# Joining the high and low part of a product's moving operand in one 512-column matmul, for three of seven products

## The reference

```python
xn = rms_norm(h, norm1_w[l])
proj = xn @ w_in[l] + b_in[l]
...
merged = jax.nn.sigmoid(gate_a) * (ya @ w_branch_a[l]) + jax.nn.sigmoid(gate_b) * (yb @ w_branch_b[l])
h = h + merged @ w_out[l]
xn2 = rms_norm(h, norm2_w[l])
h = h + (jax.nn.silu(xn2 @ w_ffn_gate[l]) * (xn2 @ w_ffn_up[l])) @ w_ffn_down[l]
```

## Time and profile before

| | |
|---|---|
| median of three runs | 816.99 us |
| profiled execution, span from first to last instruction | 815.2 us |
| TensorE busy | 808.4 us (99%), 5504 matmul records |
| VectorE busy | 539.7 us (66%), 561 instructions |
| ScalarE busy | 440.4 us (54%), 501 instructions |
| GpSimd busy | 414.0 us (51%), 146 instructions |
| granted TensorE clock | 0.999 |

### The profile page before, as it was taken

One profiled execution on the slowest core, in us unless ns is written; L12 is line 12 of the kernel. 1 busy time (PEld: TensorE's weight loads), 2 busy tenths in 40 slices (PEclk: granted clock), 3 DMA queues, 4 the chain that ended last, 5 costly groups with the idle time before them and its releaser, 6 DMA issues.

```text
span 815.2 us, 13365 instructions
## 1 busy us (share of the span) xinstructions
PE 808.4 (99%) x5504; PEld 750.1 (92%) x5504; DVE 539.7 (66%) x561; ACT 440.4 (54%) x501; POOL 414.0 (51%) x146
## 2 busy tenths in 40 slices
PE   9999999999999999999999999999999999999997
PEld 7888888888888899999998899999999999999985
DVE  5377377374674867888873278766667777677736
ACT  5523446665665645866542584454444446665624
POOL 4445424424224543477954543544444445978880
PEclk9999999999999999999999999999999999999999
DMA  7973523121123253322234203423234445535022
GB/s 294 265 263 115 164 95 104 52 104 57 52 98 115 95 204 105 104 104 105 103 130 185 104 1 107 152 106 109 106 111 159 159 152 186 178 125 212 1 78 104
DMA packets 27565, 103.11 MB, mean 126 GB/s; under 512 B 2816, under 2 KB 4224, under 8 KB 23552
## 3 DMA queue, kind: packets, MB, share of 16 engines
q1 hardware_dynamic: 22288, 87.07, 29.8%
q10 hardware_dynamic: 5232, 15.40, 5.9%
HBM read 94.08 MB, written 8.39 MB: 126 GB/s over the span
## 4 chain that ended last, share of the span: by engine, by line
PE 99%; DMA 0%; ACT 0%; issue 0%; SPq 0%; DVE 0%; ACTq 0%
PE acc L2109 14%; PE acc L2112 14%; PE acc L2111 14%; PE acc L1894 7%; PE acc L1896 6%; PE acc L1895 6%; PE acc L1913 6%; PE acc L1912 6%; PE acc L1911 6%; PE acc L2308 3%; PE acc L2307 3%; PE acc L2305 3%; PE acc L1940 3%; PE acc L2023 1%; PE acc L2062 1%; PE acc L2067 1%
## 5 line engine op out<-in xcount | busy, mean ns | idle before, releaser
L465 POOL TENSOR_TENSOR w_lo<-raw,w_hi 128x2048 fp32r<-128x2048 f32 x26 | 123.1, 4733 | 163.1 <-ACT w_hi L660 163.1
L486 POOL TENSOR_TENSOR A_lo<-wp,A_hi 128x1024 fp32r<-128x1024 f32 x51 | 126.1, 2472 | 145.6 <-ACT A_hi L833 137.3
L848 ACT ACTIVATE S_hi<-acc 128x1024 fp32r<-128x1024 f32 x68 | 68.1, 1024 | 89.5 <-PE acc L2112 56.3
L2112 PE MATMUL acc<-xt_hi,A_lo 128*128 128x256 f32 x408 | 115.5, 283 | 0.0
L2111 PE MATMUL acc<-xt_lo,A_hi 128*128 128x256 f32 x408 | 115.5, 283 | 0.0
L2109 PE MATMUL acc<-xt_hi,A_hi 128*128 128x256 f32 x408 | 115.5, 283 | 0.0
L1444 DVE TENSOR_TENSOR S_lo<-acc,S_hi 128x1024 fp32r<-128x1024 f32 x68 | 81.8, 1220 | 18.6 <-ACT S_hi L848 18.6
L1894 PE MATMUL acc<-xt_hi,w_hi 128*128 128x512 f32 (+1 forms) x240 | 92.5, 385 | 0.0
L1896 PE MATMUL acc<-xt_hi,w_lo 128*128 128x512 f32 (+1 forms) x240 | 91.7, 382 | 0.0
L1895 PE MATMUL acc<-xt_lo,w_hi 128*128 128x512 f32 (+1 forms) x240 | 91.7, 382 | 0.0
L660 ACT ACTIVATE w_hi<-raw 128x2048 fp32r<-128x2048 f32 x26 | 49.5, 1909 | 64.1 <-PE acc L1913 43.3
(11 more groups left out here) (323 smaller groups left out, 2337.6 us busy)
## 6 DMA issues: line engine op xcount, KB each, us to landing
wp<-wstream SPq DMA_DIRECT2D x34, 1024.0 KB, 6.9
raw<-wstream SPq DMA_DIRECT2D x26, 1024.0 KB, 4.8
wd<-wstream SPq DMA_DIRECT2D x16, 512.0 KB, 6.3
down_sums<-act_sum ACTq DMA_DIRECT2D x8, 512.0 KB, 3.6
sum_raw<-down_sums SPq DMA_DIRECT2D x8, 512.0 KB, 3.3
xn_in<-x ACTq DMA_DIRECT2D x4, 512.0 KB, 8.2
turned_sums<-tx ACTq DMA_DIRECT2D x4, 512.0 KB, 3.8
raw_out<-wstream SPq DMA_DIRECT2D x2, 1024.0 KB, 5.8
```

Source lines behind the costliest of these rows:

```text
L465: pool.tensor_tensor(w_lo[s][:, :], raw[s][:, :], w_hi[s][:, :], ALU.subtract).then_inc(lo_ready, 1)
L486: pool.tensor_tensor(low_of(name, rows), weights_of(name, c, rows), high_of(name, rows), ALU.subtract).then_inc(plain_low, 1)
L848: a.activation(high_of(name, rows), src, ACT.Copy).then_inc(op_high, 1)
L2112: mm = pe.matmul(dst, wl[:, g, k, :], x[0][:, k, :], start=False, stop=(k == 3), skip_group_check=True)
```

## The change

For the products S2, S3 and A22 of every pair but pair 8 (the first of the feed-forward), the two matmuls that have the same weights, high x high and high x low, become one matmul of 512 moving columns: the high part's 256 columns and the low part's 256 columns. To allow that, high and low parts are now two halves of one tensor. The result fills a whole bank for each of the two column groups: high sums in the first 256 columns, low sums in the last 256. The third matmul still has 256 columns and adds to the first half. S2 goes to banks 6 and 7 (where the weight difference stood before), S3 and A22 to banks 1 and 2, S1 and S4 to bank 3.

```diff
+            def wide_product(name, x, banks, start):
+
+                wh, wl = op_hi[name], op_lo[name]
+                for g in range(2):
+                    both = halves_of(bank[banks[g]])
+                    for k in range(4):
+                        pe.matmul(both, wh[:, g, k, :], x[:, :, k, :], start=(start and k == 0), stop=False,
+                                  skip_group_check=True)
+                        mm = pe.matmul(both[:, 0, :], wl[:, g, k, :], x[:, 0, k, :], start=False, stop=(k == 3),
+                                       skip_group_check=True)
+                mm.then_inc(product_done, 1)
...
-                product("S1", mt1, 2, True)
-
-                pe.wait_ge(s_low, 4 * p + ((2 if p == 1 else 3) - 4))
+                product("S1", mt1, 3, True)
+
+                pe.wait_ge(s_low, 4 * p - 1)
...
-                product("S2", mt2, 1, True)
+                wide_product("S2", mt2, (6, 7), True)
...
-                product("S3", mt3, 3, True)
+                wide_product("S3", mt3, (1, 2), True)
...
-                product("A22", t4, 3, False)
+                wide_product("A22", t4, (1, 2), False)
...
-                product("S4", x22, 2, False)
+                product("S4", x22, 3, False)
```

In the down pairs the weights are the moving operand, and `wide_down_product` does the same with them. The joins of these three products become two additions, the second of which waits for the first:

```diff
+            def join_wide(dst, banks, other, joins):
+
+                v.tensor_tensor(dst, low_sums(banks), other, ALU.add).then_inc(part_joined, 1)
+                v.wait_ge(part_joined, joins)
+                return v.tensor_tensor(dst, high_sums(banks), dst, ALU.add)
...
-                v.tensor_tensor(mu2[:, :], bank[1][:, :], mp1[:, :], ALU.add).then_inc(joined, 1)
+                join_wide(halves_of(mu2), SECOND_SUM, halves_of(mp1), JOINS * p + (1 - JOINS)).then_inc(joined, 1)
...
-                v.tensor_tensor(u3[:, :], bank[3][:, :], mu2[:, :], ALU.add).then_inc(joined, 1)
+                join_wide(halves_of(u3), LAST_ROW, halves_of(mu2), JOINS * p + (2 - JOINS)).then_inc(joined, 1)
...
-                merge_quarter(2, 3, mu2).then_inc(joined, 1)
+                join_wide(mcq[:, 2, :, :], LAST_ROW, halves_of(mu2), JOINS * p).then_inc(joined, 1)
```

ScalarE's copy of A21 for the next pair waits for U2's join, since it writes the banks that S2 now stands in, and the output block and the first down block wait also for c21:

```diff
+                if u2 is not None:
+                    a.wait_ge(joined, u2)
                 a.activation(row_diff if rows else diff, weights_of("A21", c, rows), ACT.Copy).then_inc(a21_copied, 1)
...
                         pe.wait_ge(taken, 2 * MERGE_PAIRS)
+                        pe.wait_ge(joined, 5 * MERGE_PAIRS - 1)
```

More of the change, by code:

```diff
@@ L97 @@
 FIRST_SUMS = 6
+JOINS = 3
 WARM_UP = 10
@@ L130, in build @@
         mt_raw = [sb(f"mt_raw{n}", 84 + 8 * n, [P, 4, HT]) for n in range(3)]
-        mt_hi = [sb(f"mt_hi{n}", 80 + 8 * n, [P, 4, HT], F32R) for n in range(3)]
-        mt_lo = [sb(f"mt_lo{n}", 84 + 8 * n, [P, 4, HT], F32R) for n in range(3)]
+        mt = [sb(f"mt{n}", 80 + 8 * n, [P, 2, 4, HT], F32R) for n in range(3)]
+        mt_hi, mt_lo = ([t[:, part, :, :] for t in mt] for part in range(2))
         mt4 = sb("mt4", 104, [P, 4, HT])
@@ L181, in build @@
         wd = [sb(f"wd{c}", 16 * c, [P, KD, HALF]) for c in range(2)]
-        row_hi = {n: sb(f"{n}_row_hi", kb, [P, 4, HT], F32R) for n, kb in SLOT.items()}
-        row_lo = {n: sb(f"{n}_row_lo", kb + 4, [P, 4, HT], F32R) for n, kb in SLOT.items()}
+        row = {n: sb(f"{n}_row", kb, [P, 2, 4, HT], F32R) for n, kb in SLOT.items()}
+        row_hi, row_lo = ({n: t[:, part, :, :] for n, t in row.items()} for part in range(2))
         def high_of(name, rows):
@@ L1078, in pair @@
                 a.wait_ge(s_low, at(p, 4, 1 - 4))
-                a21_copy(1 - c, nn, rows)
+                a21_copy(1 - c, nn, rows, None if first else at(p, 5, 1 - 5))
                 a11_high(1 - c, nn, rows)
@@ L2270, in pair @@
                     pe.wait_ge(sil_ready, 2)
-                product("S2", t2, 1, True)
+                if first:
+                    product("S2", t2, 1, True)
+                else:
+                    wide_product("S2", t2, (6, 7), True)
                 pe.wait_ge(s_low, p * 4 + (3 - 4))
@@ L2276, in pair @@
                     pe.wait_ge(act_ready, 2)
-                product("S3", t3, 3, True)
+                if first:
+                    product("S3", t3, 2, True)
+                else:
+                    wide_product("S3", t3, (1, 2), True)
                 pe.wait_ge(plain_low, p * 3 - 1)
@@ L2286, in pair @@
                     pe.wait_ge(t_low, N_LOW + 4)
-                product("A22", t4, 3, False)
+                if first:
+                    product("A22", t4, 2, False)
+                else:
+                    wide_product("A22", t4, (1, 2), False)
                 pe.wait_ge(s_low, p * 4)
                 pe.wait_ge(joined, p * 5 + (3 - 5))
-                product("S4", x22, 2, False)
+                product("S4", x22, 3, False)
             pair(MERGE_PAIRS + 1, True)
@@ L2304, in down_product, with wide_down_product @@
                     for k in range(4):
-                        pe.matmul(dst, x[0][:, k, ts], wh[:, k, :], start=(start and t == 0 and k == 0), stop=False,
+                        pe.matmul(dst, x[:, 0, k, ts], wh[:, k, :], start=(start and t == 0 and k == 0), stop=False,
                                   skip_group_check=True)
-                        pe.matmul(dst, x[0][:, k, ts], wl[:, k, :], start=False, stop=False, skip_group_check=True)
-                        mm = pe.matmul(dst, x[1][:, k, ts], wh[:, k, :], start=False, stop=(k == 3),
+                        pe.matmul(dst, x[:, 0, k, ts], wl[:, k, :], start=False, stop=False, skip_group_check=True)
+                        mm = pe.matmul(dst, x[:, 1, k, ts], wh[:, k, :], start=False, stop=(k == 3),
+                                       skip_group_check=True)
+                mm.then_inc(product_done, 1)
+            def wide_down_product(name, x, banks, start):
+                for t in range(2):
+                    both = halves_of(bank[banks[t]])
+                    ts = slice(t * P, (t + 1) * P)
+                    for k in range(4):
+                        pe.matmul(both, x[:, 0, k, ts], row[name][:, :, k, :], start=(start and k == 0), stop=False,
+                                  skip_group_check=True)
+                        mm = pe.matmul(both[:, 0, :], x[:, 1, k, ts], row_hi[name][:, k, :], start=False, stop=(k == 3),
                                        skip_group_check=True)
```

96 lines of the change are left out of this document (56 added, 40 removed).

## The result

The changed kernel took 827.6 us (median of 4 runs, 826.46 to 830.36) against 816.93 us for the kernel before on the same chip (816.86 to 817.32). The ratio is 1.013, with a 95% interval of 1.0115 to 1.0145: 10.7 us slower, where 6.4 us were worked out and 823.0 was forecast. The direction was right. The time lies 0.1 us outside the range given, and 4.6 us above the forecast.

The account below looks back on a forecast made before the run. TensorE was taken to bound the kernel, with 99% of the chain of waits. 816.99 us plus 12.8 of stalls less 6.4 saved gave 823.4, rounded down to 823.0; range 817.5 to 827.5.

Parts of the forecast that it names:

- The saving, 6.4 us: In 60 wide products on TensorE, 16 matmuls replace 24, each product 0.107 us shorter; bounds 0 and 6.4 us.
- the operand's jump: Wide matmuls' two-piece moving operand might stream at a cost that eats the fixed 13 ns per matmul, lowering the saving.
- The stalls, 12.8 us: TensorE's waits for VectorE's 60 added join additions, summed over all places to 12.8 us; bounds 9 and 15.5.
- merge pair 2: Behind this pair, which forms three sums with no VectorE idle time, TensorE stalls 1.9 us more than before.
- pairs 3 and 4: Merge pairs with two extra VectorE instructions each: stalls of 0.80 and 0.92 us, 1.7 us together.
- FFN pairs with sums: Four FFN pairs forming activation sums: stalls of 0.94, 0.81, 0.81 and 0.94 us, 3.5 us together.
- last pair: A22 waits 0.8 us for u3's later end; c21 before the last down blocks costs another 0.6 us.
- The steady pairs: Pairs without extra work, and A22 in the loop's four pairs: small late waits, 1.3 us together, bounds 0 and 2.5.
- The rule for a late wait: At a late wait, the matmul starts 0.15 us after VectorE's end and the second matmul comes another 0.07 late.
- If the granted clock fell in the gaps: A sign that would show the forecast wrong: TensorE's clock falling in its idle gaps; no size was given.
- the saving is small: Rival: the jump between operand pieces costs 10 of 13 ns, so wide products save 1.6 us: 828.2 us; chance 0.05.
- The saving wins: Rival: VectorE catches up at longer rests in pairs with extra work; stalls of 3 us give 813.6 us; chance 0.09.

Follow-up runs that it names:

- experiment 2: Changed kernel with each wide product's join as one addition of the high sums, low sums left out of the output: 814.18 us.
- experiment 8: As experiment 7, but in pair 19 two GpSimd operations wait until VectorE's low parts are done: 834.48 us.
- experiment 3: As experiment 2, but high and low columns lie side by side for three of four moving operands, making one 512-column piece: 814.19 us.
- experiment 7: Changed kernel with merge pair 2's first two refill sums and four FFN pairs' activation sums moved ahead of the second sum's join: 836.33 us.
- experiment 10: Changed kernel with only the second sum's product wide, merge pair 5 all narrow, sums in their place: 816.58 us.
- experiment 5: As experiment 2, but the low weights' matmul also moves 512 columns, so wide products have one width: 862.52 us, one run.

## Why the prediction missed

- **The saving, 6.4 us: this step failed.** It measured 2.85 us (experiment 2), and 3.55 of the 4.6 us between forecast and result are here; with 2.85 in its place the forecast would have been 826.6, inside its range. That VectorE's joins cost more than the matmuls save was right; of the two terms of the sum this one was mis-sized. The step put together 0.2267 us for a 512-column matmul, read where all neighbours have 512 columns, and 0.12 for one of 256, read where all have 256. The product that was built mixes them, and a pair takes 0.353. The price was bounded from both sides, 0 and 6.4, with the operand's jump as the only reason for less; I then took an end of the range. By the formula of the Trainium skill ("TensorE: Matmul & The Clock Gate", Back-to-back issue gap), N/2.4 plus 2.5 ns for a matmul by itself, the saving would be an estimated 1.2 us. The measured 5.9 ns for each instruction lie between its 2.5 and the 13 of the rows, nearer to the former. The formula gives 109 ns for a narrow one, and the 0.12 of the trace stands against that.
- **The stalls, 12.8 us: right in sum, partly by luck.** The changed kernel's own trace has 11.54 us in stalls and 1.04 for the second matmuls, 12.6 in all. Place by place, forecast and trace: merge pair 2 1.9 and 2.05; pairs 3 and 4 0.80 and 0.92, 0.72 and 0.91; pair 5 1.6 and 1.54; output block 0.7 and 0.55; FFN pairs with sums 3.5 and 3.0; last pair 0.8 and 0.36, and nothing over 0.12 where c21 was to cost 0.6 ahead of the down blocks. Against these overestimates stands the place that was missed, pair 19 to 20, 1.90 + 0.52. I had followed the FFN pairs and taken the down pairs for steady ones, without reading that pair 19 has two low parts ahead of c21, as the FFN pairs have their two sums. The mechanism there was missed too: the additions moved these low parts against GpSimd's work, which made them 1.8 us longer (5.75 against 3.92), and experiment 8 shows that the 1.90 came from that. The steady pairs, taken at 1.3 us, showed under 0.1 each: those of the FFN loop start 19.99 to 20.07 us apart, within the 19.84 to 20.1 that were forecast, where the kernel with single joins has 19.98 to 19.99.
- **The rule for a late wait** (0.15 us from VectorE's end to the matmul, 0.07 at the second one) held: in the gap behind merge pair 2 the matmul starts 0.15 behind VectorE's end and the second one 0.19 behind the first again. In the FFN pairs the second came 0.10 late and not 0.07.
- **The clock, left out.** "If the granted clock fell in the gaps" stood among the things that would make it wrong, without a price. It fell to 0.51 for 3.2 us behind the 2.05 us gap, which cost 1.5 us in the profiled execution.
- **The sum now**, for the profiled execution: 816.93 + 12.6 - 2.85 + 1.5 = 828.2, and it took 828.0. The median of the four runs is 827.6.
- **The rival "the saving is small"** (828.2, chance 0.05) had the best number, by luck: its saving of 1.6 us was 1.25 too small and it had no term for the clock, and the two nearly cancel. Its mechanism, the operand's two pieces, fell with experiment 3. "The saving wins" asked that VectorE catch up at its rests, and experiment 7 shows what such a rest is worth while GpSimd has work in it.

## What to carry to other kernels

Read the price of an instruction where its neighbours look as they will in the changed kernel; put together from two pure stretches, the saving came out at more than twice the real one here. An instruction saved on the bounding engine at 6 ns each can't pay for 0.7 us of work on an engine whose result is due in every pair: count the slack at each place where the bound engine waits, in all kinds of pairs, and price additions only as far as they run over it (in the FFN pairs with sums one of 0.69 us was free and three cost 0.7 to 0.8). Before work is moved into an engine's idle time, look at what GpSimd does in that time, since the two took turns here.

## What the runs showed of the hardware

- VectorE's operations of 128x1024 with all operands in SBUF and GpSimd's exclude each other: 1.22 us alone, 1.6 to 3.4 when issued during one of GpSimd's, ending 1.08 us after it; GpSimd's 2.41 becomes 2.8 to 3.4 when it is issued during one of VectorE's. VectorE's operations that read PSUM kept their 1.22 beside GpSimd's (L1441 at 736.67, with GpSimd at work from 732.30 to 741.79). The kernel before had it too: the low parts of pair 19 took 1.61 and 2.31 us there.
- TensorE's granted clock fell to about a half for some 3 us at or behind gaps of 2.05, 2.41, 2.47 and 2.48 us, behind one of 2.6 us ahead of the pairs in experiment 10, and at one of two gaps near 2.8 us (2.76 in experiment 7, while behind 2.77 in experiment 8 it stayed at 1.00). It stayed up behind 1.92, 1.90 and 1.81 us. The fall cost some 1.5 us each time.
- Matmuls of 512 and 256 columns in turn: 0.353 us for the two; of one width 0.227 and 0.120. Behind narrow ones the first five wide ones took 0.228 to 0.236, and 0.227 from the sixth on (experiment 5).
